# The substitution steps of a triangular inverse, moved from VectorE to GpSimd, with one store moved behind them

## The reference

```
def step(s, inp):                      # RWKV-7, per token
    r_t, w_t, k_t, v_t, a_t, b_t = inp
    sa = jnp.einsum('bhij,bhj->bhi', s, a_t)
    s = s * w_t[:, :, None, :] + sa[..., None] * b_t[:, :, None, :] + v_t[..., None] * k_t[:, :, None, :]
    return s, jnp.einsum('bhij,bhj->bhi', s, r_t)
```

## Time and profile before

| | us |
|---|---|
| median of 3 runs (lowest, highest) | 1511.07 (1499.93, 1514.33) |
| the profiled execution | 1496.55 |
| its span, first to last instruction | 1494.7 |
| TensorE busy | 1277.8 (85% of the span) |
| VectorE busy | 670.6 (45%) |
| ScalarE busy | 309.2 (21%) |
| GpSimd busy | 154.7 (10%) |
| mean granted TensorE clock | 0.935 of full |

### The profile page before, as it was taken

One profiled execution on the slowest core, in us unless ns is written; L12 is line 12 of the kernel. 1 busy time (PEld: TensorE's weight loads), 2 busy tenths in 40 slices (PEclk: granted clock), 3 DMA queues, 4 the chain that ended last, 5 costly groups with the idle time before them and its releaser, 6 DMA issues.

```text
span 1494.7 us, 14647 instructions
## 1 busy us (share of the span) xinstructions
PE 1277.8 (85%) x5643; PEld 774.8 (52%) x5643; DVE 670.6 (45%) x1327; ACT 309.2 (21%) x576; POOL 154.7 (10%) x172
## 2 busy tenths in 40 slices
PE   2699988997899978998889799549999999999772
PEld 1245567665786667665774355234444444444330
DVE  4516763389426864388435956530111111111176
ACT  2213322233214222224113000101111111111212
POOL 3100100010000000010002232200000000000053
PEclk9899998999999999999989989759999999999976
DMA  9554210011001110013014111055888888888562
GB/s 348 177 190 177 73 29 1 14 43 43 1 1 30 41 29 1 14 29 129 1 45 170 71 64 53 16 207 214 336 330 334 329 335 333 337 334 335 181 228 99
DMA packets 55615, 213.94 MB, mean 143 GB/s; under 512 B 23401, under 2 KB 23609, under 8 KB 44041
## 3 DMA queue, kind: packets, MB, share of 16 engines
q1 hardware_dynamic: 41912, 167.29, 31.2%
q0 software_dynamic: 8320, 28.49, 5.2%
q10 hardware_dynamic: 5328, 17.41, 2.9%
HBM read 184.19 MB, written 29.01 MB: 143 GB/s over the span
## 4 chain that ended last, share of the span: by engine, by line
PE 68%; DVE 22%; ACT 3%; DMA 3%; issue 3%; POOL 1%; ACTq 0%; POOLq 0%; SPq 0%; DVEq 0%
PE ps L1092 15%; PE ps L718 13%; PE ps L1103 7%; PE ps L1009 7%; PE ps L841 6%; DVE arena L1621 3%; DVE arena L1623 3%; ACT arena L1381 2%; PE ps L1087 2%; PE ps L934 2%; PE ps L941 2%; PE ps L943 1%; PE ps L879 1%; PE ps L935 1%; PE ps L684 1%
## 5 line engine op out<-in xcount | busy, mean ns | idle before, releaser
L718 PE MATMUL ps<-arena 128*128 128x348 f32 (+5 forms) x1056 | 320.9, 460 | 4.6 <-DVE arena L1507 4.6
L718 PEld LDWEIGHTS ps<-arena 128*128 128x128 f32 (+2 forms) x1056 | 194.2, 187 | 127.3 <-issue 27.9
L1092 PE MATMUL ps<-arena 128*128 128x512 f32 x512 | 231.1, 605 | 29.7 <-ACT arena L1381 29.7
L1092 PEld LDWEIGHTS ps<-arena 128*128 128x128 f32 x512 | 95.7, 192 | 146.3 <-issue 125.8
L1971 DVE TENSOR_TENSOR arena<-arena,ps 128x256 f32<-128x256 f32 x32 | 13.5, 422 | 282.0 <-ACT arena L1386 282.0
L1009 PE MATMUL ps<-arena 128*128 128x512 f32 (+1 forms) x288 | 130.9, 610 | 0.0
L1103 PE MATMUL ps<-arena 128*128 128x512 f32 x256 | 115.2, 592 | 1.1 <-ACT arena L1390 1.1
L841 PE MATMUL ps<-arena 128*128 128x128 f32 (+3 forms) x768 | 88.1, 294 | 1.1 <-ACT arena L1294 1.1
L1009 PEld LDWEIGHTS ps<-arena 128*128 128x128 f32 (+1 forms) x288 | 52.1, 185 | 67.4 <-issue 67.3
L841 PEld LDWEIGHTS ps<-arena 128*128 128x128 f32 (+2 forms) x768 | 81.6, 193 | 7.8 <-issue 2.7
L1103 PEld LDWEIGHTS ps<-arena 128*128 128x128 f32 x256 | 48.6, 190 | 62.1 <-issue 60.7
(11 more groups left out here) (382 smaller groups left out, 1657.4 us busy)
## 6 DMA issues: line engine op xcount, KB each, us to landing
arena<-in_w_gu SPq DMA_DIRECT2D x32, 2048.0 KB, 11.9
arena<-in_w_dn SPq DMA_DIRECT2D x32, 1024.0 KB, 5.3
arena<-in_w_ada SPq DMA_DIRECT2D x24, 1024.0 KB, 5.1
slot_scr<-arena ACTq DMA_DIRECT2D x32, 512.0 KB, 11.7
arena<-in_w_in SPq DMA_DIRECT2D x20, 512.0 KB, 3.8
arena<-in_x_all SPq DMA_DIRECT2D x16, 512.0 KB, 10.5
arena<-in_w_out SPq DMA_DIRECT2D x8, 512.0 KB, 6.8
h_scr<-arena SPq DMA_DIRECT2D x8, 512.0 KB, 3.1
```

What stands on the lines that cost most here:

```text
L718: mm = T.matmul(ps[0:rows, c, 0:w], lhs(k), hT[:, k, c0:c0 + w], start=(k == 0), stop=(k == KC - 1))
L1092: mm = T.matmul(ps[:, 2 + b, :], xgt[b][:, k, :], exgu[b][:, k, :], start=(k == 0), stop=(k == KC - 1))
```

## The change

The 60 instructions of the substitution are issued by GpSimd (`G`) instead of VectorE (`V`), in the same order, on the same tiles, each linked to the one before. They follow directly on the select and the memset. `solved` is raised once a block, behind the last step, so SyncE waits for `j + 1`. GpSimd's wait for the recurrent rows and the store to `conv_o` come behind the steps instead of ahead of the wait for the lanes. VectorE goes from the convolution straight to the wait for the values.

```diff
@@ SyncE
-                sp.wait_ge(HV["solved"], 2 * j + 2)
+                sp.wait_ge(HV["solved"], j + 1)
@@ GpSimd
                 link(G.memset(pinv_flat, 0.0))
-                pool.wait_ge(win_out, 6 + 15 * j + 9)
-                pool.dma_start(conv_o[j], prec[:, PAD + SEQ - 3:PAD + NTOK]).then_inc(outs, 16)
                 pool.wait_ge(lane_in, 80 * (j + 1))
                 m = lanes.rearrange("l (s t) -> l s t", t=32)
                 select(m, [[-1, 32], [1, 32]], ALU.is_gt, 0, 0)
-                G.memset(lanes[:, 0:1024:33], 1.0).then_inc(HV["solved"], 1)
+                link(G.memset(lanes[:, 0:1024:33], 1.0))
+                for k in range(1, 31):
+                    w = 31 - k
+                    prod = lane_tmp[:, 0:k * w].rearrange("l (s t) -> l s t", t=w)
+                    link(G.tensor_tensor(prod, m[:, 0:k, k:k + 1].to_broadcast([64, k, w]),
+                                         m[:, k:k + 1, k + 1:32].to_broadcast([64, k, w]), ALU.mult))
+                    last = G.tensor_tensor(m[:, 0:k, k + 1:32], m[:, 0:k, k + 1:32], prod, ALU.add)
+                    if k < 30:
+                        link(last)
+                last.then_inc(HV["solved"], 1)
+                pool.wait_ge(win_out, 6 + 15 * j + 9)
+                pool.dma_start(conv_o[j], prec[:, PAD + SEQ - 3:PAD + NTOK]).then_inc(outs, 16)
@@ VectorE
-                dve.wait_ge(HV["solved"], 2 * j + 1)
-                m = lanes.rearrange("l (s t) -> l s t", t=32)
-                for k in range(1, 31):
...
-                last.then_inc(HV["solved"], 1)
                 dve.wait_ge(win_out, 6 + 15 * j + 12)
                 link(shift_tile(2, pv, MU_V))
```

## The result

| | before | changed |
|---|---|---|
| median of 11 runs | 1503.44 us (1498.13 to 1514.33) | 1518.62 us (1516.27 to 1519.36) |
| profiled execution (span) | 1496.55 (1494.7) | 1517.67 (1515.7) |
| mean granted clock in it | 0.935 | 0.921 |

The ratio is 1.009, with a 95% interval of 1.0065 to 1.0115: slower, the direction that was forecast, but by 15 us instead of 24. In the prediction's own classes, with their border at 1%, these 0.9% fall into "same", to which it gave 0.23, and not into "slower" (0.68). The three runs that the prediction saw had their median at 1511.07; with eleven it is 1503.44. The profiled executions are 21 us apart.

The account below looks back on a forecast made before the run. The substitution in VectorE's program order, then TensorE's own work, was taken as the bound; +15.1 us for u_mm's shift and 9.2 for the clock gave +24, 1521 on the profiled execution, 1535 on the median; range 1498 to 1600.

Parts of the forecast that it names:

- the shift of `u_mm`: Later start of u_mm on TensorE: +5.7 us in block 0, +3.15 in blocks 1 and 2, +3.1 in 3; together +15.1.
- break-even: Rival: steps and waits sum to 39 to 43 us, clock not lost, within 15 us of 1511; chance 0.20 plus 0.03.
- What bounds: VectorE's program order makes the substitution late; u_mm also waits for its result through pinv, so the later path counts.
- The bound on a gain: TensorE's gate projection and Gram products come next, so a block gains at most some 6.6 us, not 22.
- The steps: The 60 substitution instructions on GpSimd, 9920 elements a block: 36.8 us by the low line, 50.2 by the high.
- My line: Low line for GpSimd's two-input instructions: 2.08 ns per element and 0.20 us fixed, through 1.26 and 2.33 us.
- The rival with 0.53 us fixed: GpSimd's small steps have a high fixed cost: steps 50.2 us, kernel 1557, or 1613 if no waits hide; chance 0.26.
- The waits between the engines: VectorE and GpSimd stop each other beside the steps: 5.8 us in block 0, 8.7 in the others.
- The start of `u_mm` before: u_mm taken to start when the first akv_out copy ends: 207.42, 374.95 and 708.37 in blocks 0, 1 and 3.
- TensorE's clock: New wait before the first 96 solve products lowers the granted clock: 2.3 us a block, 9.2 us; bounds 0 and 9.2.
- Costs of nothing: Moved projected-rows store, SP's weight and w_out loads, mod_scr rows, state loads and convolution may slip without delaying their readers.
- The rival of a faster kernel: Engines don't hold each other up and freed VectorE wins: 1494 us, or 1485 with still shorter steps; chance 0.09.

Follow-up runs that it names:

- the experiment with half the steps: Changed kernel with steps 16 to 30 left out, so the inverse is incomplete: 1475.52 us, ratio 0.9816 to the kernel before.
- the store experiment: Changed kernel with the conv_o store back in front of the wait for the lanes, steps still on GpSimd: 1527.39 us, ratio 1.0158 to the kernel before.

## Why the prediction was off in size

The direction, the mechanism and the order of the paths were right. The size was not: +24 us forecast, +15 measured. The term that failed is the shift of `u_mm`, 15.1 us in the sum and 7.4 in the traces, and in it the length of the steps above all. Besides, the base to which the sum was added was 8 us too high. The time fell into the range of *break-even* (within 15 us of 1511), but not by its reasons: steps and waits took 43.9 us in three of the blocks, not 39 to 43, and the clock was lost.

- **What bounds** (right). TensorE's `u_mm` waits for the later of two paths, and after the change that is `pinv` in all four blocks, 6.9 to 7.3 us behind the last step (384.29 - 377.33 in block 1; 7.0 forecast). The bound on a gain, 6.6 us a block, was 7 in the experiment with half the steps.
- **The steps** (36.8 us, the step that failed most). Alone they take 34.7 us. The small instructions run from 0.23 us at 30 elements to 0.61 at 240 on L596. My line, drawn through 512 elements on 128 partitions and 1024 on 8, gave 0.26 and 0.70. The rival with 0.53 us fixed is out. That is 2.1 us a block too much, 8.4 in all; `u_mm` sits behind it at full price, as the store experiment shows.
- **The waits between the engines** (5.8 and 8.7 us, nearly right): 6.9 and 9.2. Too little by 1.1 and three times 0.5, 2.6 us in all. That they came so near is partly luck: two of the instructions counted as not waiting do wait (L1632), and of the 19 counted for block 0 the sum used 18.
- **The start of `u_mm` before** (207.42, 374.95 and 708.37, misread). It is 0.48 us later, so the shift is smaller by 1.9 us over four blocks.
- **The path in sum**: 15.1 - 8.4 + 2.6 - 1.9 = 7.4 us, which is the 7.4 read from the four blocks.
- **TensorE's clock** (9.2 us, nearly right). I charged the whole difference between two stretches of 96 products, 2.3 us, in each block. The 80 products behind the new wait take 10.19, 10.26, 10.45 and 10.39 us. Before, the same 80 took 8.26 in block 1, at the upper level, as this view of the kernel before says (the clock is the 1.00):

```profile
375.43:383.69 8.26, 8.26 (x83) 7.47 (x83) 2.53 (x5) 2.78 (x5) 0.00 (x0) 1.00 0.01 2
```

  So the wait costs these products 8.3 us in all. Where the second half's products begin 7.3 us of it are left: from `u_mm` to there the changed kernel takes 39.1 us in each block, and the execution from which I predicted took 37.0, 37.2, 37.5 and 37.5.
- **The base.** 7.4 + 7.3 = 14.7 us from the traces, beside 15.2 between the medians. The profiled executions differ by 21 us, since that of before was among its fastest: the other 6.3 us lie 1.4 ahead of the first lanes' load and the rest from the second-half products of block 2 on, where the kernel before lost 8 us itself in its execution of 1508.23 us. I moved the sum to the median of three, 1511.07, which eight more runs put 8 us lower. The forecast time of 1535 misses by 16 us, of which this base is 8, the path 8 and the clock less than 1.
- **Costs of nothing** held: no later reader waited for the moved store, for `w_out` or for `mod_scr`. But the store was worth a gain that I had not counted by itself: 9 us with the steps on GpSimd, 5 with them on VectorE.

The rival of a faster kernel fell by the waits that were measured, the rival of a high fixed cost by the size of the steps.

## What to carry to other kernels

Before moving a chain of small instructions from VectorE to GpSimd, count the instructions beside it on VectorE, first those that read two SBUF tiles: here each side paid for the other, and of 6.3 us of steps that were shared out VectorE paid 4.0 back. Find the second reader of the moved result; it may bound the gain long before the freed engine does. Where other products stand ahead of a product on TensorE, date it by its own first record and not by the copy that it waits for. And don't add a sum to the median of three runs when single runs differ by 1%: here eight more moved it by 8 us.

## What the runs showed of the hardware that I had not expected

- The kernel before varies by 1.3% from run to run, in step with the mean granted clock (1495 us at 0.933, 1515 at 0.922). The changed kernel, and that with the store in front, in which TensorE waits for `pinv` in every block, are slower but vary by 0.2%. Why is open.
- GpSimd's two-input fp32 instructions on short rows of a triangle cost about what a straight line gives. The products (L596) take 0.23 us at 30 elements, 0.44 at 150 and 0.61 at 240, which is 1.8 ns per element and 0.18 us fixed; the additions (L598) reach 0.69 at 240.
- A short GpSimd instruction beside VectorE's scan is four times as long as alone (1.18 us against 0.28). It began 0.2 us behind the start of the scan's first instruction, which took 1.23 us, and ended 0.2 us behind its end.
